# Expert block: weight tiles fetched two at a time into paired buffers, and the gate split made in place

## The reference

```python
def block(hc):                                    # 128 tokens at a time
    q = (hc @ wq).reshape(128, 8, 2, 128)         # 8 heads, two half queries each
    sc = einsum('thcd,hckd->thck', q, keys)       # 128 keys per half
    s1, i1 = top_k(sc[:, :, 0], 16); s2, i2 = top_k(sc[:, :, 1], 16)
    cand = s1[..., :, None] + s2[..., None, :]    # 256 sums, the best 16 are chosen
    top, pos = top_k(cand, 16); eidx = i1 * 128 + i2 (taken at pos)
    gate = softmax(top)
    act = gelu(einsum('thkd,td->thk', u_tab[eidx], hc))
    return einsum('thk,thkd->td', gate * act, v_tab[eidx])
```

## Time and profile before

| what | value |
|---|---|
| median of three runs | 3953.64 us |
| profiled execution, device time | 3949.28 us |
| its span | 3947.6 us |
| TensorE matmul busy | 3674.9 us, 93% |
| TensorE weight load busy | 3355.1 us, 85% |
| VectorE busy | 2938.7 us, 74% |
| ScalarE busy | 1352.4 us, 34% |
| GpSimd busy | 732.9 us, 19% |
| DMA, mean over the span | 222 GB/s |
| granted TensorE clock, mean | 0.972 of full speed |

### The profile page before, as it was taken

How to read it: one execution, slowest core, us unless ns; L and a number is a source line. 1 busy time by engine, 2 the same in 40 slices (tenths; PEclk the granted TensorE clock), 3 DMA queues, 4 the chain that set the end, 5 groups by cost and what they waited for, 6 DMA issues and landing times. The chain is left out here.

```text
span 3947.6 us, 69568 instructions
## 1 busy us (share of the span) xinstructions
PE 3674.9 (93%) x28586; PEld 3355.1 (85%) x28586; DVE 2938.7 (74%) x5404; ACT 1352.4 (34%) x2055; POOL 732.9 (19%) x592
## 2 busy tenths in 40 slices
PE   8798889899999989999989988989999999999998
PEld 5568767799999989999976776769999898999998
DVE  7566454588998977877766645458898897778876
ACT  3431233333334433333333123333333443333332
POOL 2000000022121132433410000002222112234431
PEclk9899899999999999999999998999999999999999
DMA  7721221387886899999942031227778688999995
GB/s 235 264 73 45 72 91 59 99 265 249 255 256 236 298 342 319 350 338 345 341 169 70 3 115 50 90 90 254 247 251 259 230 298 333 317 349 338 347 347 189
DMA packets 322781, 876.27 MB, mean 222 GB/s; under 512 B 29696, under 2 KB 158848, under 8 KB 315680
## 3 DMA queue, kind: packets, MB, share of 16 engines
q1 hardware_dynamic: 248736, 603.36, 45.1%
q0 software_dynamic: 73728, 268.47, 18.8%
HBM read 746.93 MB, written 124.78 MB: 221 GB/s over the span
## 5 line engine op out<-in xcount | busy, mean ns | idle before, releaser
L217 PE MATMUL peer_ps<-peer_h_high,tile_high 128*128 128x384 f32 (+1 forms) x2304 | 798.8, 347 | 63.0 <-ACT up_act L2342 23.0
L219 PE MATMUL peer_ps<-peer_h_high,tile_low 128*128 128x384 f32 (+1 forms) x2304 | 789.1, 342 | 0.0
L218 PE MATMUL peer_ps<-peer_h_low,tile_high 128*128 128x384 f32 (+1 forms) x2304 | 788.8, 342 | 0.0
L210 DVE TENSOR_TENSOR tile_low<-tile,tile_high 128x1024 fp32r<-128x1024 f32 x544 | 662.8, 1221 | 165.6 <-ACT tile_high L205 150.8
L217 PE MATMUL peer_ps<-gate_high,tile_high 128*128 128x384 f32 x2048 | 693.8, 339 | 29.5 <-DVE tile_low L210 29.3
L218 PE MATMUL peer_ps<-gate_low,tile_high 128*128 128x384 f32 x2048 | 691.3, 338 | 0.0
L219 PE MATMUL peer_ps<-gate_high,tile_low 128*128 128x384 f32 x2048 | 691.1, 337 | 0.0
L2222 POOL DMA_INDIRECT row<-in_peer_u_rows,row_at x256 | 314.5, 1229 | 1789.5 <-DVE row L2466 1064.1
L205 ACT ACTIVATE tile_high<-tile 128x1024 fp32r<-128x1024 f32 x544 | 571.0, 1050 | 32.2 <-DMA tile<-in_peer_u 31.8
L217 PEld LDWEIGHTS peer_ps<-peer_h_high,tile_high 128*128 128x128 f32 x2304 | 435.5, 189 | 90.5 <-issue 48.2
L2222 POOL DMA_INDIRECT row<-in_peer_v,row_at x256 | 391.9, 1531 | 636.5 <-DVE own_sum L2472 564.6
(11 more groups left out here) (480 smaller groups left out, 5200.1 us busy)
## 6 DMA issues: line engine op xcount, KB each, us to landing
tile<-in_peer_u SPq DMA_DIRECT2D x256, 512.0 KB, 4.6
tile<-in_peer_v SPq DMA_DIRECT2D x256, 512.0 KB, 6.3
gates<-gates_out SPq DMA_DIRECT2D x24, 2048.0 KB, 10.5
gates_in<-gates SPq DMA_DIRECT2D x32, 1536.0 KB, 14.5
acts<-up_act SPq DMA_DIRECT2D x240, 192.0 KB, 5.1
act_in<-acts SPq DMA_DIRECT2D x240, 192.0 KB, 6.4
in_w<-in_w_in SPq DMA_DIRECT2D x36, 512.0 KB, 3.3
tile<-in_peer_wq SPq DMA_DIRECT2D x32, 512.0 KB, 4.2
```

Source lines behind the costliest of these rows:

```text
L210: return dve.tensor_tensor(out, value, high.bitcast(F32), ALU.subtract)
L217: pe.matmul(out, wh, mh, start=first, stop=False)
L218: pe.matmul(out, wh, ml, start=False, stop=False)
L219: return pe.matmul(out, wl, mh, start=False, stop=last)
```

## The change

Query, up and down tiles are laid out in DRAM in pairs: for each partition the row of the even tile is followed by that of the odd tile, 8 KB in all. SBUF has two pair buffers (four tiles, 16 KB per partition) where it had three tile buffers (12 KB). SyncE issues a load at even m only; it fetches both tiles, signals one semaphore per pair, and waits for `tile_low` of both tiles of the pair before the last one. The order of everything else in SyncE's queue stays. The gathered rows of the down table come from a separate DRAM array in the old layout, `peer_v_rows`. `share_gates` overwrites `gate_row` and has no buffer `left`.

```diff
-NRAW, NSPLIT, NPS = 3, 3, 2
+NSPLIT, NPS = 3, 2
+NPAIR = 2
...
-    dram_rows = (pg.dram["peer_u_rows"], pg.dram["peer_v"].rearrange("l e p d -> (l e p) d"))
+    dram_rows = (pg.dram["peer_u_rows"], pg.dram["peer_v_rows"])
...
-        raw = [buf(f"tile{b}", [P, D]) for b in range(NRAW)]
+        raw_pair = [buf(f"tile{b}", [P, 2 * D]) for b in range(NPAIR)]
+        raw = lambda m: raw_pair[m // 2 % NPAIR][:, m % 2 * D:(m % 2 + 1) * D]
...
             def load(m):
-                if m >= NRAW:
-                    sp.wait_ge(low_made.sem, low_made.at(m - NRAW + 1))
+                j = m // 2
+                if j >= NPAIR:
+                    sp.wait_ge(low_made.sem, low_made.at(2 * (j - NPAIR) + 2))
                 kind, i = STREAM[m] if m < UPS else ("v", DOWN[m - UPS])
-                source = queries[i] if kind == "q" else tables[int(kind == "v")][i]
-                sp.dma_start(raw[m % NRAW][:, :], source).then_inc(loaded[m % NRAW].sem, 16)
+                source = queries[i // 2] if kind == "q" else tables[int(kind == "v")][i // 2]
+                sp.dma_start(raw_pair[j % NPAIR][:, :], source).then_inc(loaded[j % NPAIR].sem, 16)
...
-            for m in range(UPS + NRAW):
-                load(m)
+            for m in range(UPS + NSPLIT):
+                if m % 2 == 0:
+                    load(m)
...
-            for e in range(NRAW, NKEY):
+            for e in range(NSPLIT, NKEY):
                 if KEPT <= e + 2 < NKEY:
                     load_act(e + 2 - KEPT)
-                load(UPS + e)
+                if e % 2 == 0:
+                    load(UPS + e)
...
             def high(m):
-                act.wait_ge(loaded[m % NRAW].sem, loaded[m % NRAW].at(16 * (m // NRAW + 1)))
+                j = m // 2
+                act.wait_ge(loaded[j % NPAIR].sem, loaded[j % NPAIR].at(16 * (j // NPAIR + 1)))
...
             def share_gates():
-                link(dve.tensor_tensor(left[:, :], gate_row[:, :], route[:, 2, :], ALU.subtract))
-                link(dve.tensor_copy(route[:, 3, :], left[:, :]))
-                link(dve.tensor_tensor(left[:, :], left[:, :], route[:, 3, :], ALU.subtract))
-                link(dve.tensor_copy(route[:, 4, :], left[:, :]))
+                for j in (2, 3):
+                    link(dve.tensor_tensor(gate_row[:, :], gate_row[:, :], route[:, j, :], ALU.subtract))
+                    link(dve.tensor_copy(route[:, j + 1, :], gate_row[:, :]))
...
+    def in_pairs(w):
+        n = w.shape[1] // 2
+        return w.reshape(L, n, 2, P, D).transpose(0, 1, 3, 2, 4).reshape(L, n, P, 2 * D)
```

More of the change, by code:

```diff
@@ L2080, in peer @@
     U32 = mybir.dt.uint32
-    loaded = [pg.counts(f"tile_loaded{b}") for b in range(NRAW)]
+    loaded = [pg.counts(f"tile_loaded{b}") for b in range(NPAIR)]
     high_made, low_made = pg.counts("tile_high_made"), pg.counts("tile_low_made")
@@ L2142, in peer @@
             key_ramp = buf("key_ramp", [P, NKEY, 2], BF16, own=own)
-            left = buf("gates_left", [P, TD], own=own)
             spill = [buf(f"gates_out{b}", [P, NKEY, SPILL], own=own) for b in range(2)]
@@ L2203, in _ @@
                     load_slab(1)
-            for m in range(UPS + NRAW - late, UPS):
+            for m in range(UPS + NSPLIT - late, UPS):
                 store(m)
-            for e in range(NRAW, NKEY):
+            for e in range(NSPLIT, NKEY):
                 if KEPT <= e + 2 < NKEY:
                     load_act(e + 2 - KEPT)
-                load(UPS + e)
-                s = (e - NRAW) // SLAB + NSLAB
-                if (e - NRAW) % SLAB == SLAB - 1 and s < SLABS:
+                if e % 2 == 0:
+                    load(UPS + e)
+                s = (e - NSPLIT) // SLAB + NSLAB
+                if (e - NSPLIT) % SLAB == SLAB - 1 and s < SLABS:
                     load_slab(s)
@@ L2326, in high @@
                     split_high(act, gh[m % NSPLIT][:, :], mixed[m % 2][:, :])
-                split_high(act, wh[m % NSPLIT][:, :], raw[m % NRAW][:, :]).then_inc(high_made.sem, 1)
+                split_high(act, wh[m % NSPLIT][:, :], raw(m)).then_inc(high_made.sem, 1)
             def take(m):
@@ L2422, in lows @@
                     dve.wait_ge(high_made.sem, high_made.at(m + 1))
-                    split_low(dve, wl[m % NSPLIT][:, :], raw[m % NRAW][:, :], wh[m % NSPLIT][:, :]).then_inc(low_made.sem, 1)
+                    split_low(dve, wl[m % NSPLIT][:, :], raw(m), wh[m % NSPLIT][:, :]).then_inc(low_made.sem, 1)
                     done[0] = m + 1
@@ L2646, in _ @@
             dve.wait_ge(added.sem, added.at(1))
-    for m in range(UPS + NKEY):
-        loaded[m % NRAW].passed(16)
+    for j in range((UPS + NKEY) // 2):
+        loaded[j % NPAIR].passed(16)
     for s, n in ((high_made, UPS + NKEY), (low_made, UPS + NKEY), (summed, UPS + NKEY), (taken, UPS), (keys_loaded, 16),
@@ L2741 @@
         "xa_wv": rows(a["xa_wv"]),
-        "peer_wq": tiles(a["peer_wq"]),
+        "peer_wq": in_pairs(tiles(a["peer_wq"])),
         "peer_keys": a["peer_keys"].reshape(L, 2 * PH, NKEY, P).transpose(0, 3, 1, 2),
-        "peer_u": experts(a["peer_u"]).reshape(L, NKEY, NKEY, KD, P).transpose(0, 1, 4, 3, 2).reshape(L, NKEY, P, D),
+        "peer_u": in_pairs(experts(a["peer_u"]).reshape(L, NKEY, NKEY, KD, P).transpose(0, 1, 4, 3, 2).reshape(L, NKEY, P, D)),
         "peer_u_rows": experts(a["peer_u"]).reshape(L * NKEY * NKEY, D),
-        "peer_v": experts(a["peer_v"]),
+        "peer_v": in_pairs(experts(a["peer_v"])), "peer_v_rows": experts(a["peer_v"]).reshape(L * NKEY * NKEY, D),
     }
```

## The result

The changed kernel takes 4058.14 us as median of four runs (4047.5 to 4069.6), the kernel before 3958.86 beside it. The ratio is 1.0248, with a 95% interval of 1.0222 to 1.0273: 2.5% slower. The direction was the forecast's, the size was four times the forecast's.

What follows compares the result with a forecast made beforehand. TensorE sets the pace, its waits of 69 us, 1.7% of the span, being the most to gain. The profiled 3949.3 + 38 (stores) - 8 (turn) - 6 (down) = 3973.3 us, as median 3978; range 3938 to 4012.

Steps and rivals of the forecast that it cites:

- The tile that lands later: Even tile's load brings 1 MB instead of 512 KB: 1.3 us longer, but the up tile itself stays covered.
- The stores behind the load: Up part: even activation stores queue behind 1 MB and land 1.3 us later; 19 us per layer, +38 us in both.
- The odd stores: Up part: they follow no load and land 1.3 us sooner; about 5 us per layer of TensorE's waits go.
- The run of tiles 86 to 103: Up part, tiles 86 to 101: saturated chain with 8 even takes, 7 intervals of 1.3 us, 9 us per layer.
- The turn: From up to down: slab 0 starts some 4.5 us sooner, TensorE's wait falls by about 4 per layer, -8 in all.
- The down part: Odd tile goes ahead of the slab, next pair waits behind it; small gain, -6 us, bounds -29 and +36.
- What costs nothing: Fewer tile issues on SyncE, first pair's landing, `share_gates` in place and gathered rows from another array: covered but for 0.3 us.
- the stores not held: Up part: load's second half overlaps the store, or the odd chain's relief carries both; 3929 us, chance 0.16.
- a cancelling gain: Up part: the odd chain's gain eats two thirds of the even one's price, up +14; 3954 us, chance 0.21.
- cheaper large transfers: Tile loads: larger transfers save fixed cost, so waits at the turn and in the down part go; 3908 us, chance 0.05.
- The slab rival: Down part: pairs behind each of 28 slabs come 1.3 us late, +36 beside the stores' cost; 4020 us, chance 0.08.
- the signs that I had named: If right: heads' take waits 25 us or more per layer, store landings split 2.5 us apart, tiles 85 to 96 take 5.4.

Runs made afterwards that it cites:

- single buffers with both cures: Four single tile buffers in place of pairs, activation store issued ahead of the load, each slab from the third on fetched in four parts: 3875.43 us, ratio 0.9813.
- the last kernel with pairs: The changed kernel with the activation store ahead of the pair load and each slab from the third on fetched in four parts: 3890.52 us, ratio 0.9827.
- the store first: The changed kernel with the up part's activation store of tile m-6 issued ahead of the pair load at each even m: 3940.7 us, ratio 0.9956.
- The split slabs: Each gate slab from the third on fetched in four parts behind successive tiles: four single buffers 3881.26 us, the changed kernel with pairs 4006.52 us.
- the small parts: The kernel before with only the gate split in place and the gathered down rows from their own array: 3954.33 us, ratio 0.9987.

## Why the prediction was right or wrong

**What bounds it** was read rightly: TensorE's waits were the stake, with the store chain and the slabs at their two ends. But the 69 us that I called the most that a better tile stream could give are not the most: single buffers with both cures took off 77 us (3875.43 against 3952.15 beside them). The lower clock behind a wait goes with the wait, and I had not counted it.

**The tile that lands later** costs nothing by itself in the heads and the down part: the last kernel with pairs shows it. The added time of the second half was right, 1.3 us forecast, 1.2 measured at the stores' median.

**The stores behind the load** is the step that failed, in size. Forecast +38 us; heads, run and gates together gave +83.8. These terms of the sum were wrong:
- The even takes of the heads. 2.2 us per head were forecast, 30 us in both layers; the waits at even takes came to 46.0, from 0.5.
- The lower clock behind each of these waits had no term in the sum. It gave the better part of the other 21 us of the heads.
- The gate groups. I put them at nothing, as covered. They gave +21.6 us. With the store first all but 3.2 of these are gone (432.2 against 429.0), so it is the same chain, in a queue that holds a store of 2 MB of gates as well. It reaches TensorE by way of VectorE: TensorE waits for one-hot planes 5.3 and 6.0 us, VectorE for `tile_high`, which ScalarE makes behind a take, 12.7 and 10.8 us (4.9 and 7.7 before). With the turn, which they shortened, they gave +9.1.
- The odd stores. I wrote that they follow no load and land 1.3 us sooner. They are issued right behind the 1 MB and land 1.4 us later (6.5 against 5.1); I had overlooked that the even iteration's wait holds both. The sum was not hurt by it: the 10 us that I took off for waits at odd takes did go (12.4 to nothing), as those takes now follow a later even one.

The run of tiles 86 to 103, on which I had built the term, was the part that fell short: 9 us per layer forecast, 3.8 measured. I had read its pace from the starts of the takes of tiles 85 to 96, 4.93 us each. By the same measure it is 5.25 after, near the 5.4 that I had named. TensorE's own starts there were 4.6 us apart before and 4.9 after: the takes fell behind TensorE within the stretch, so it was held less than I had said.

**The turn** was right in kind, -8 forecast, -12.5 measured, and in size partly by luck: with the store first, where TensorE arrives on time, the same pairs gain 3.4 (68.2 against 71.6). The 12.5 stand against the 21.6 of the gate groups ahead.

**The down part** was wrong in sign: -6 forecast, +18.3 measured, 10 of it in waits. I set the bytes behind a slab against the due time of the next tile and found a small gain; the bound of +36 held it. The split slabs show that the mechanism was the named one, a pair that stands whole behind a slab, and that its price was above the gain of the odd tile that goes ahead. And of the 29 us of waits on which I worked, 7.3 belong to the first down tile of each layer and stand in every kernel.

**What costs nothing** held: the small parts measured 0.9987. The 9.3 us outside the block, in code that the change doesn't touch, are not explained. That sum is 1350 to 1360 us in most of these kernels and 1347 in two of them, so it may be no more than the spread between executions; that stays open.

The rivals of the stores not held, of a cancelling gain and of cheaper large transfers were refuted by the result, and the first two by the store first as well. The slab rival was in the right at half its price, beside the main one and not in its place. Of the signs that I had named, the landings did not split into two groups: both rose. The range was too narrow because I bounded each term around its middle value, although my own bounds allowed +112 for the stores.

## What to carry to other kernels

Doubling a transfer doubles what stands ahead of everything issued behind it: look in the queue for the small store or load that gates an engine, and issue it first. Set the time from when its data is ready to when it lands against the time until its buffer is asked for again; a small delay costs nothing until the two meet. Here a deeper ring was worth its memory when its buffers were freed and asked for one by one, and in pairs only once nothing urgent stood behind them. Split the rare large transfer that all the frequent ones must pass. The store first alone, with no further buffer, took the old kernel 1.0% lower; both steps with the memory of a fourth tile took it 1.7 (pairs) and 1.9% (singles) lower, of which the fourth single buffer by itself gave 1.8.

## What the runs showed of the hardware

- A wait of TensorE of 2.86 us was followed by ten microseconds at a mean granted clock of 0.66, with 1.00 before it. In the heads 33 us of added waits made the stretches 54.5 us longer. A stall costs more than its length.
- The same bytes in two transfers of 512 KB, in pieces of 4 KB, cost 30 us more than in one of 1 MB in pieces of 8 KB (39 us between the profiled executions, with 15.8 us of it in the heads and 19.7 in the down part). Whether the size of the pieces or the number of transfers does it was not tried apart.
- Behind a slab of 1.5 MB the next issue of SyncE took 3.14 us, behind a part of 384 KB 0.32 us: in the two places looked at, the issuing engine was held behind the large one, as by a queue that is full.
